# mLSTM tail of a two-stack decoder kernel: numerators copied out by ScalarE, quotient in place, level sums cleared at the stage's entry

## What is computed

```
mLSTM:  num = (scores * w_intra) @ v + inter-chunk part
        den = sum(scores * w_intra) + inter-chunk part
        h   = num / maximum(abs(den), exp(-m))
HGRN2:  o_t = sum over s<=t of (q_t * prod of decays s+1..t * k_s) v_s
out   = concat(norm(h) * sigmoid(mo), norm(o) * silu(hg), attention) @ w_out
```

## Time and profile before

| | |
|---|---|
| median of 3 runs | 3514.96 us (3513.9 to 3518.54) |
| profiled execution | 3513.15 us, of it the span 3511.1 us |
| TensorE busy | 3154.8 us (90%) |
| VectorE busy | 1886.4 us (54%) |
| ScalarE busy | 1255.6 us (36%) |
| GpSimd busy | 398.8 us (11%) |
| mean granted TensorE clock | 0.946 of full speed |

### The profile page before, as it was taken

The page is one execution under the profiler, slowest core; times in us unless marked ns, Lnnn a source line. Parts: engine busy times, 40 slices in busy tenths (PEclk is TensorE's granted clock), DMA queues, the critical chain, the costliest instruction groups (busy, mean ns, idle before and its releaser), DMA issues.

```text
span 3511.1 us, 37316 instructions
## 1 busy us (share of the span) xinstructions
PE 3154.8 (90%) x14560; PEld 2454.3 (70%) x14560; DVE 1886.4 (54%) x2608; ACT 1255.6 (36%) x1997; POOL 398.8 (11%) x281
## 2 busy tenths in 40 slices
PE   6788799998879799998999797999979987979997
PEld 4566688887566688886666765888756557668886
DVE  6575544458575544457665546444577635464445
ACT  4444322234434422243444333222333423332222
POOL 2120200013021200003001302000110012020001
PEclk9888899999988899999999999999999989999998
DMA  3110122322110223222111311222211113122222
GB/s 118 41 37 19 66 96 97 97 94 90 37 42 19 69 89 97 96 97 77 55 49 66 103 60 61 98 99 97 90 42 55 48 60 107 37 78 97 96 96 78
DMA packets 72650, 259.07 MB, mean 74 GB/s; under 512 B 7908, under 2 KB 10088, under 8 KB 71976
## 3 DMA queue, kind: packets, MB, share of 16 engines
q1 hardware_dynamic: 71672, 252.73, 21.6%
q0 software_dynamic: 816, 4.13, 0.3%
HBM read 254.73 MB, written 2.10 MB: 73 GB/s over the span
## 4 chain that ended last, share of the span: by engine, by line
PE 50%; issue 28%; DVE 10%; ACT 4%; POOLq 3%; DVEq 3%; POOL 1%; DMA 0%; ACTq 0%; SPq 0%
PE bank L485 37%; POOLq L2483 3%; DVE w_lo L1725 2%; PE bank L968 2%; ACT w_hi L1135 1%; PE bank L979 1%; DVEq L1971 1%; DVE h_d L1981 1%; PE bank L546 1%; PE bank L989 1%; PE bank L534 1%; PE bank L1005 1%; PE bank L993 1%; PE bank L512 1%; PE bank L733 1%
## 5 line engine op out<-in xcount | busy, mean ns | idle before, releaser
L485 PE MATMUL bank<-a_hi,w_hi 128*128 128x512 f32 x2040 | 832.3, 408 | 112.3 <-DVE a_lo L1755 47.6
L1725 DVE TENSOR_TENSOR w_lo<-w_raw,w_hi 128x1024 fp32r<-128x1024 f32 (+1 forms) x474 | 621.5, 1312 | 360.4 <-ACT w_hi L1135 358.9
L485 PE MATMUL bank<-a_lo,w_hi 128*128 128x512 f32 x2040 | 805.7, 395 | 0.0
L485 PE MATMUL bank<-a_hi,w_lo 128*128 128x512 f32 x2040 | 805.4, 395 | 0.0
L485 PE MATMUL bank<-b_hi,w_hi 128*128 128x512 f32 (+1 forms) x1688 | 652.6, 387 | 74.1 <-DVE w_lo L1725 38.5
L485 PE MATMUL bank<-b_lo,w_hi 128*128 128x512 f32 (+1 forms) x1688 | 642.6, 381 | 0.0
L485 PE MATMUL bank<-b_hi,w_lo 128*128 128x512 f32 (+1 forms) x1688 | 641.0, 380 | 0.0
L1135 ACT ACTIVATE w_hi<-w_raw 128x1024 fp32r<-128x1024 f32 (+1 forms) x474 | 493.6, 1043 | 402.2 <-DMA w_raw<-weights 402.2
L485 PEld LDWEIGHTS bank<-a_hi,w_hi 128*128 128x128 f32 x2040 | 390.1, 191 | 228.9 <-issue 80.3
L485 PEld LDWEIGHTS bank<-a_lo,w_hi 128*128 128x128 f32 x2040 | 390.8, 192 | 85.3 <-issue 7.6
L485 PEld LDWEIGHTS bank<-a_hi,w_lo 128*128 128x128 f32 x2040 | 389.8, 191 | 84.3
(11 more groups left out here) (275 smaller groups left out, 3106.2 us busy)
## 6 DMA issues: line engine op xcount, KB each, us to landing
w_raw<-weights SPq DMA_DIRECT2D x458, 512.0 KB, 3.4
w_raw<-weights SPq DMA_DIRECT2D x16, 384.0 KB, 3.0
x<-x SPq DMA_DIRECT2D x1, 2048.0 KB, 9.6
mem<-mem POOLq DMA_DIRECT2D x2, 1024.0 KB, 5.1
out<-x SPq DMA_DIRECT2D x8, 256.0 KB, 2.0
mem<-mem SPq DMA_DIRECT2D x1, 1024.0 KB, 15.3
ple<-ple POOLq DMA_DIRECT2D x2, 512.0 KB, 3.8
pos_i<-positions POOLq DMA_DIRECT2D x2, 256.0 KB, 6.7
```

Source lines behind the costliest of these rows:

```text
L485: last = mm(bank[G_BANK[u % 4] if at is None else at][:, 0:cols], w[:, u % SLOTS, ks], t[:, k, 0:cols], start=(k == 0 and n == 0), stop=(k ...
L1725: tt(w_lo[:, u % SLOTS, w], w_raw[:, u % SLOTS, w], f32(w_hi[:, u % SLOTS, w]), ALU.subtract).then_inc(w_lo_ready, 1)
```

## The change

ScalarE's `denominators` also copies the two numerators out of banks 6 and 7 into `o` and only then signals `m_den_made`. VectorE's quotient is one instruction in place in `o`. TensorE waits for `m_den_made` where it waited for `m_ended`. The tile `m_w` is split in two that lie elsewhere (bytes 16 to 20 KB and 28 to 32 KB of the region), so that `h_d` shares none with it; in return the first exponentials that write there (`level_exps(1)`) wait for the last sums. GpSimd clears `h_d` as soon as the first projection tile of the layer is finished, ahead of its wait for `h_f_made`.

```
-        m_w = inner("m_w", [P, 2, 2, S], 20)
+        m_w_even, m_w_odd = inner("m_w_even", [P, 2, S], 16), inner("m_w_odd", [P, 2, S], 28)
+        m_w = [(m_w_even[n], m_w_odd[n]) for n in range(LAYERS)]
...
                     if i == 4:
-                        pe.wait_ge(m_ended, 2 * l + 1)
+                        pe.wait_ge(m_den_made, 2 * l + 1)
...
-                pe.wait_ge(m_ended, 2 * (l + 1))
+                pe.wait_ge(m_den_made, 2 * (l + 1))
                 turn_tile(T_HI, 6)
...
                     f(m_den[0:64, p, :], bank[6][64:128, :], ACT.Abs)
-                    f(m_den[64:128, p, :], bank[7][0:64, :], ACT.Abs).then_inc(m_den_made, 1)
+                    f(m_den[64:128, p, :], bank[7][0:64, :], ACT.Abs)
+                    f(o[0:64, p, :], bank[6][0:64, :], ACT.Copy)
+                    f(o[64:128, p, :], bank[7][64:128, :], ACT.Copy).then_inc(m_den_made, 1)
 
                 def level_exps(lev):
+                    if lev == 1:
+                        act.wait_ge(m_summed, 16 * (l + 1))
...
-                    tt(o[0:64, p, :], bank[6][0:64, :], m_den[0:64, p, :], ALU.mult)
-                    tt(o[64:128, p, :], bank[7][64:128, :], m_den[64:128, p, :], ALU.mult)
+                    tt(o[:, p, :], o[:, p, :], m_den[:, p, :], ALU.mult)
                     dve.drain().then_inc(m_ended, 1)
...
+                pool.wait_ge(t_made, WIN_T * l + 1)
+                pool.memset(h_d[l][:, :, :, :], 0.0).then_inc(h_zeroed, 1)
                 pool.wait_ge(h_f_made, l + 1)
                 pool.memset(h_ls[l][:, :, :], 0.0).then_inc(h_started, 1)
-                pool.wait_ge(m_summed, 16 * (l + 1))
-                pool.memset(h_d[l][:, :, :, :], 0.0).then_inc(h_zeroed, 1)
```

More of the change, by code:

```diff
@@ L665, in sums @@
                     if i == 4:
-                        pe.wait_ge(m_ended, 2 * l + 1)
+                        pe.wait_ge(m_den_made, 2 * l + 1)
                     for e in range(2):
-                        mm(bank[6 + e][:, j * P:], v[:, j, qs(2 * p + e)], m_w[l][:, i % 2, e, j * P:],
+                        mm(bank[6 + e][:, j * P:], v[:, j, qs(2 * p + e)], m_w[l][i % 2][:, e, j * P:],
                            start=(j == 0), stop=(j == 3)).then_inc(m_summed, 1)
@@ L1320, in exps @@
                         k = 4 * j + 2 * p + e
-                        f(m_w[l][:, i % 2, e, j * P:], bank[4 + e][:, j * P:], ACT.Exp, bias=m_col[:, k:k + 1],
+                        f(m_w[l][i % 2][:, e, j * P:], bank[4 + e][:, j * P:], ACT.Exp, bias=m_col[:, k:k + 1],
                           scale=-1.0).then_inc(m_w_made, 1)
@@ L1931, in block @@
                     for e in range(2):
-                        d = m_w[l][:, i % 2, e, qs(j)]
+                        d = m_w[l][i % 2][:, e, qs(j)]
                         stt(d, d, 1.0, tri, ALU.min, ALU.mult)
@@ L1935, in block @@
                     for e in range(2):
-                        w = m_w[l][:, i % 2, e, j * P:]
+                        w = m_w[l][i % 2][:, e, j * P:]
                         dve.wait_ge(m_scored, 2 * (8 * l + i) + e + 1)
```

## The result

| | before | after |
|---|---|---|
| median | 3514.81 us | 3524.78 us |
| range, runs | 3512.96 to 3522.11, 14 | 3521.62 to 3526.45, 14 |
| profiled execution | 3513.15 us | 3521.62 us |
| its span | 3511.1 us | 3519.8 us |

The ratio is 1.0023 (1.0015 to 1.0032). The change makes the kernel slower by 0.23%, 10 us on the medians, where I gave 3516.9 us and a chance of 0.89 for no change. The point, the range (up to 3521.5) and the likeliest class were all wrong. The profiled execution of after is its fastest run; it is 8.5 us over the one of before.

The account below looks back on a forecast made before the run. It took waits in the mixer, through ScalarE, VectorE and GpSimd to TensorE, as what the change could move. Layer 0's 1.00 plus layer 1's 0.96 gave +1.96 us on 3514.96: 3516.9 us, range 3512.5 to 3521.5.

Parts of the forecast that it names:

- Copies, second pair: ScalarE's two copies delay level 0 exponentials and scores 1.2 us; net +0.83 us in layer 0, +0.79 in layer 1.
- the clock at no cost: Longer TensorE waits ahead of the level 0 scores cost 0 through the clock in both layers; bounds -1 to +5.
- Rival A: Longer wait before level 0 scores loses the clock through scores, half and transposes: +7.9 us, 3522.8; chance 0.08.
- First pair: Copies start VectorE's larger-of 0.87 us later, merged quotient saves 0.70: block 4 starts 0.17 us later, in both layers.
- The clearing at the entry: GpSimd's clearing of `h_d`, some 100 us earlier, slows VectorE beside it by 0 to 0.5 us a layer; taken as 0.
- VectorE rows at the stage's entry that grew: Sign that the forecast was wrong: the new place of the clearing hurts, +0.5 us a layer.
- the rival: New place of the `h_d` clearing hurts VectorE at the stage's entry: +0.5 us a layer on top, 3517.9; chance 0.07.
- rival B: ScalarE's copies cost next to nothing on the chain, so the saved waits stay: -2.2 us, 3512.8; chance 0.08.

Follow-up runs that it names:

- trimmed before: Before with two VectorE drains fewer in each layer, one in each of two `recips` calls, nothing of the change: median 3521.14 us (1.0011).
- the clearing alone: Before with `m_w` split and `h_d` cleared at the stage's entry; no copies, old quotients and TensorE waits: median 3519.18 us (1.0002).
- before with the exponentials first: Before with ScalarE's level 0 exponentials moved ahead of the second pair's absolute values, nothing else: median 3513.98 us (0.9992).
- kernel with the copies behind the exponentials: After with `h_d` cleared in its old place, two opening drains, second pair's absolute values signalled separately and its copies behind level 0 exponentials: median 3508.85 us (0.9981).
- both padded kernels: After, and after with the clearing of `h_d` in its old place, each with two drains added in VectorE's opening: medians 3522.9 and 3522.02 us.
- copies alone: After with the clearing of `h_d` back in its old place behind the last sums: median 3521.22 us (1.0011).
- behind `h_ls`: After with the clearing of `h_d` directly behind that of `h_ls`: median 3521.3 us (1.0011).
- cleared twice: After with `h_d` cleared twice in a row at the stage's entry: median 3529.14 us (1.0042).
- padded after: After with two more drains in VectorE's opening: median 3522.9 us (1.0015).
- the clearing on the best version: The best version with `h_d` cleared at the stage's entry: median 3508.63 us (0.9976).
- copies padded: After with the clearing of `h_d` in its old place and two drains in VectorE's opening: median 3522.02 us (1.0012).
- the best version: After with second pair's absolute values, then copies (own semaphore), behind level 0 exponentials, `h_d` cleared in its old place, two opening drains: median 3507.91 us (0.9973).

## Why the prediction was wrong, step by step

**Copies, second pair: mechanism right, size short.** I had +1.20 from last sums to scores; +1.21 and +1.20 came, in every kernel with copies in front. I had the scores and the half behind them at 6.64 us, taking the place of a pinned 7.00. Before, trimmed before and the clearing alone all show 7.00 there, and so does before with the exponentials first, whose scores took 1.99 us instead of 3.59: VectorE's quotient decides. With copies in front TensorE decides, and its time depends on the clock: 6.2 to 7.7 us. In layer 0 of after it is 7.67. The scores took 3.79, and the next matmuls of the half still took 0.63 apiece, against 0.40 at its end. The waits themselves came as 5.72 and 4.90 us where I had 4.26 and 5.56: the scores started when I said, but the half ahead of them ran at another clock and ended earlier or later. So 1.9 and 1.1 us were added from last sums to transposes (16.37 and 16.38 became 18.25 and 17.49), where I had 0.8 and 0.8. Part of that came back: from the start of the level 1 scores to that of the level 8 scores layer 0 took 86.2 us, and 88.1 before. The step that failed here is the clock at no cost, where it made the 0.8 and 0.8 into 1.9 and 1.1; both lie inside the bounds of -1 to +5 that I gave it. Rival A was half there: the slow level outlasted the scores in layer 0, but not the whole half, nor the transposes.

The Trainium skill (TensorE: Matmul & The Clock Gate, "Why this matters for your kernels") advises against idle gaps between bursts of matmuls. The trace agrees on this gap, with scores of 3.79 us behind a wait of 5.72 and of 2.06 behind one of 1.40, but the length of the wait does not settle it: with the exponentials first there are scores of 2.0 us behind a wait of 2.04 and of 3.27 behind one of 1.95.

**First pair: right in layer 0.** Step 3's sums to last sums: 32.65 us in after, 32.47 to 32.54 in the kernels without copies other than before itself. That is +0.1 to +0.2, as I had worked out (+0.17); the wait ahead of the larger-of is there with 0.77. Before itself has 31.55, about 1 us less, with none of these changes to explain it; it also has 1.4 less in the steps at 106 to 122 us, which ran at a granted clock of 1.00 in before and of 0.91 in after. Some 2.4 us of the 8.7 between the two profiled spans are thus not of the change. The kernel with the copies behind the exponentials is the one other trace with that short stretch (14.5 us, the rest 15.8 to 16.3). In layer 1 the copies brought either 0 (after, both padded kernels) or +0.95 (copies alone, behind `h_ls`, cleared twice).

**The clearing at the entry: a step that failed.** "I take 0, because that neighbour read SBUF on GpSimd and a clearing doesn't": that holds for a `TENSOR_TENSOR` (the larger-of beside the clearings stayed 0.69) and is false for what stands here. I read the price off a `TENSOR_TENSOR` beside GpSimd, and what stands at the entry is a `TENSOR_SCALAR`. It was held for 1.2 us (1.67 against 0.48), over twice my upper bound of 0.5, and passed 0.8 and 1.2 us on to the next low part. What TensorE loses by that hangs on the clock behind the wait. Over 849 to 903 us after lost 2.3 us, and cleared twice 2.9; the clearing alone, the padded after and the clearing on the best version have the same 1.67 and lost nothing there (53.8 each), since TensorE's next wait there got shorter (3.75 us in the padded after, 5.36 in the copies alone) and the matmuls behind it ran at the full clock; behind the same wait of 3.78 in after they didn't. I had even asked for "VectorE rows at the stage's entry that grew"; the rival was right in kind and too small.

The Trainium skill (SBUF — State Buffer, "Who interferes with whom") says that VectorE's copies and `tensor_scalar`, in their two-port modes, share a port pair with GpSimd under an exclusive lock, and that whichever starts first keeps it for the whole instruction. The trace agrees: the 1.67 us instruction began 0.41 behind the clearing and ended 0.27 behind it, and the 1.95 beside the second clearing also ended 0.27 behind it. I had not weighed that rule.

**An edge I never looked for: the number of VectorE's instructions.** The merged quotient makes VectorE's queue shorter by one for each pair, and that alone is tied to the 3.0 us at 820 us. In all 14 kernels the order went with the count: the eight whose low part stands where it stood before got the quick order behind the 0.45 us pause, the six that are two short did not. Before with two drains less reproduces it without the change. What makes the pause is not shown. The runs show that it stands ahead of this product when the product is VectorE's 773rd instruction, and is absent when the same product is the 771st.

**How they add up.** As means over before in the same comparison: copies alone +3.9, clearing alone +1.4, shorter queue alone +3.6, copies padded +3.8, after padded +5.6, after about +8. Parts of near 2.8 us for the copies, 2.3 for the clearing and 2.1 for the order fit these within about 1.5. The prediction had 2.0, 0 and 0. So by this fit most of the excess over my 2.0 comes from the two things that I had at nothing, the clearing and VectorE's count, and only a small part from the copies' size. The steps that failed are thus these: the clearing at 0, where it held an instruction for 1.2 us in each layer; no term for VectorE's count, where 3.0 us went with it in the MLP of layer 0; and the clock at 0, where it added 1.1 and 0.3 us to the two second pairs.

**What stays open.** The split is no better than 1 to 2 us a part: e.g. the padding gave 1.9 on after and 2.5 on the best version, but nothing on the copies alone, and the clearing cost nothing that the total shows on the best version while twice the clearing cost 4.4 on after, more than its 1.5 a layer. The clock explains part of both: single stretches that no edit touches moved by 1.4 to 3.1 us between traces. The clock's scatter is as large as what is sought, with before itself spread over 3512.6 to 3524.0. And why the copies behind the exponentials give 7 us, not the 2.2 of rival B, I can name only in part. The absolute values' early signal comes with a shorter first pair, 31.2 and 30.8 us in layer 0 in place of the others' 32.5 to 32.7, and 30.9 in layer 1 in place of 31.7 or more. Last sums to transposes take 15.8 and 16.3 in place of 16.4 and 16.4. That early signal was never run without moving the copies, so how much of the 7 us is its own is not shown.

## What to carry to other kernels

An engine that takes its work in order makes everything behind an added instruction wait, so ask for each added one who is waiting for the next in that queue: with the same two copies ahead of the exponentials the kernel was 3.8 us slower than before, and with those of the second pair behind them, and the absolute values signalled at once, 7 us faster. When a wait is taken off a fast engine, work out what decides next and at which clock it will run. Look for stretches that no edit touches and that moved all the same: here they moved by as much as the parts of the change. And before a large clearing is moved to a place that looks idle on its own engine, read which instructions of VectorE stand beside it, operation by operation.

## What was new about the hardware

- A GpSimd clearing of 128x2048 (1.8 us) holds a `TENSOR_SCALAR` of VectorE on only 4 partitions until it ends: 0.48 to 1.67 us, and 0.42 to 1.95 for the next when cleared twice. It does nothing to a reciprocal of 3.35 us.
- Where `TENSOR_TENSOR` of VectorE and of GpSimd, inputs in SBUF, meet, the one that came second is slowed: a low part takes 1.22 us and GpSimd's addition 2.20 in one order, 2.23 and 1.30 in the other. In these traces a kernel with the second order takes 3.0 us longer over the MLP of layer 0.
- Two drains in VectorE's opening, some 800 us ahead, go with the order: in 14 traces of 14 it follows the number of VectorE's instructions. By the total, adding them gave 1.9 and 2.5 us (3524.78 to 3522.9, and 3510.4 to 3507.9, with intervals that overlap) and nothing on the copies alone; taking them away cost 3.6.
- One stretch of layer 1's attention, the same in all kernels, took 22.1 to 22.3 us at a granted clock of 0.92 in ten traces and 25.2 at 0.73 in four.
- A copy of 64x512 out of a bank takes 0.59 us, the same as 128x512: half the partitions save nothing on ScalarE.
